# Spatial gating in fp16 halves, and the latents' squares added on VectorE ahead of one fp32 product

## The reference, cut to what matters

```
def _rmsnorm(x, g):
    xf = x.astype(jnp.float32)
    y = xf * lax.rsqrt(jnp.mean(xf * xf, -1, keepdims=True) + EPS)
    return (y * g.astype(jnp.float32)).astype(x.dtype)
...
def _gmlp(u, v, ln_g, ln_b, ws, bs):
    u = jax.nn.gelu(u)
    v = _layernorm(jax.nn.gelu(v), ln_g, ln_b)
    w = jnp.where(jnp.tril(jnp.ones((L, L), dtype=bool)), ws[:, :L, :L], 0).astype(v.dtype)
    vc = v.reshape(B, nc, L, GMLP_GROUPS, GMLP_DG)
    sp = jnp.einsum('gts,bcsgd->bctgd', w, vc) + bs[:, :L].T[:, :, None].astype(v.dtype)
    return u * sp.reshape(B, T, GMLP_WIDTH), v
```

## Time and profile before

| | |
|---|---|
| median of the timed runs | 997.51 us |
| the profiled execution's own time | 998.19 us |
| its span, first to last instruction | 996.3 us |
| TensorE busy | 959.4 us (96%) |
| VectorE busy | 823.3 us (83%) |
| ScalarE busy | 673.0 us (68%) |
| mean granted TensorE clock | 0.996 |

### The profile page before, as it was taken

The page is one execution under the profiler, slowest core; times in us unless marked ns, Lnnn a source line. Parts: engine busy times, 40 slices in busy tenths (PEclk is TensorE's granted clock), DMA queues, the critical chain, the costliest instruction groups (busy, mean ns, idle before and its releaser), DMA issues.

```text
span 996.3 us, 24157 instructions
## 1 busy us (share of the span) xinstructions
PE 959.4 (96%) x9862; PEld 748.8 (75%) x9862; DVE 823.3 (83%) x1484; ACT 673.0 (68%) x1092; POOL 0.7 (0%) x10
## 2 busy tenths in 40 slices
PE   9999999999999899999999999999999989999994
PEld 7877777777776799965578777777777768999652
DVE  6796767776789899998888876678768889999986
ACT  7665555866365899886677545568653659998764
POOL 0000000000000000000000000000000000000000
PEclk9999999999999999999999999999999999999998
DMA  9855444323564299998736544443344425999951
GB/s 366 335 170 160 136 152 129 130 86 128 169 221 141 87 368 379 379 364 299 265 108 233 175 121 142 154 130 95 119 146 151 155 79 177 384 374 397 367 208 56
DMA packets 59651, 205.01 MB, mean 206 GB/s; under 512 B 7216, under 2 KB 10348, under 8 KB 59020
## 3 DMA queue, kind: packets, MB, share of 16 engines
q1 hardware_dynamic: 56748, 198.08, 57.1%
q10 hardware_dynamic: 2784, 5.28, 1.6%
HBM read 198.76 MB, written 3.40 MB: 203 GB/s over the span
## 4 chain that ended last, share of the span: by engine, by line
PE 65%; DVE 18%; ACT 8%; issue 5%; DVEq 2%; DMA 1%; ACTq 0%; SPq 0%
PE bank L1880 42%; DVE wlo L1135 9%; PE bank L1904 4%; ACT whi L593 4%; PE bank L2425 3%; DVE xT L1148 2%; PE bank L1909 1%; PE bank L2242 1%; DVE xlo L1154 1%; PE bank L2441 1%; PE bank L1949 1%; DVEq L1186 1%; PE bank L2174 1%; DVE mu_var L1187 1%; PE bank L2345 1%
## 5 line engine op out<-in xcount | busy, mean ns | idle before, releaser
L1135 DVE SCALAR_TENSOR_TENSOR wlo<-w,whi 128x1024 f16<-128x1024 f32 x358 | 428.1, 1217 | 61.5 <-ACT whi L593 60.2
L593 ACT ACTIVATE whi<-w 128x1024 f16<-128x1024 f32 x358 | 370.0, 1050 | 79.2 <-PE bank L1880 52.9
L1880 PE MATMUL bank<-xhi,whi 128*128 128x320 f16 x688 | 206.1, 300 | 0.8 <-DVE wlo L1135 0.8
L1880 PE MATMUL bank<-xhi,wlo 128*128 128x320 f16 x688 | 205.7, 299 | 0.0
L1880 PE MATMUL bank<-xlo,whi 128*128 128x320 f16 x688 | 205.7, 299 | 0.0
L1880 PE MATMUL bank<-arena_b,whi 128*128 128x112 f16 x2048 | 159.4, 213 | 3.4 <-DVE wlo L1135 3.2
L1880 PE MATMUL bank<-arena_b,wlo 128*128 128x112 f16 x1024 | 156.0, 213 | 0.0
L1880 PEld LDWEIGHTS bank<-arena_b,whi 128*128 128x128 f16 x2048 | 149.8, 98 | 5.3 <-issue 3.1
L1880 PEld LDWEIGHTS bank<-arena_b,wlo 128*128 128x128 f16 x1024 | 100.2, 98 | 0.4 <-issue 0.4
L1880 PEld LDWEIGHTS bank<-xhi,whi 128*128 128x128 f16 x688 | 67.2, 98 | 28.5 <-DVE wlo L1135 1.1
L1880 PEld LDWEIGHTS bank<-xhi,wlo 128*128 128x128 f16 x688 | 67.3, 98 | 26.2
(11 more groups left out here) (377 smaller groups left out, 1755.2 us busy)
## 6 DMA issues: line engine op xcount, KB each, us to landing
w<-in_w SPq DMA_DIRECT2D x358, 512.0 KB, 5.0
arena_b<-head_rows ACTq DMA_DIRECT2D x2, 1920.0 KB, 9.8
rows<-in_rows SPq DMA_DIRECT2D x2, 1024.0 KB, 10.0
xT<-in_x SPq DMA_DIRECT2D x2, 640.0 KB, 5.5
out_y<-xT SPq DMA_DIRECT2D x4, 320.0 KB
out_ckv<-arena_a SPq DMA_DIRECT2D x2, 320.0 KB
acc<-kr SPq DMA_DIRECT2D x2, 288.0 KB
arena_c<-kr SPq DMA_DIRECT2D x2, 288.0 KB
```

What stands on the lines that cost most here:

```text
L593: A(whi[:, n % SLOTS, :], w32[:, n % RAW, :], ACT.Copy, scale=WS).then_inc(hi_done.sem, 1)
L1135: V.scalar_tensor_tensor(wlo[:, n % SLOTS, :], w32[:, n % RAW, :], WS, whi[:, n % SLOTS, :], ALU.mult, ALU.subtract).then_inc(lo_done.sem, 1)
L1880: ins = M(out, w[:, s, sub * P:(sub + 1) * P], rhs(part, k), start=(n == 0), stop=(n == 3 * len(subs) - 1))
```

## The change

There are two parts. In the front, DVE adds the two squares of each latent into one tile, and TensorE does one fp32 product for each latent in place of two; it waits for the new signal `sq_s`. The additions stand at the head of DVE's loop over the token blocks. In the heads, `ws_t` is split once a layer into `ws_hi` and `ws_lo` (after the mask), and `vg` for each head into `vg_hi` and `vg_lo`; TensorE does nine fp16 products in place of three fp32 ones. ACT makes `vg_hi` ahead of `hi_m(5)`, and DVE makes `vg_lo` behind `lo_m(5)`. The bias is now added with the scale 1/256 in the same instruction.

```diff
@@ latents_hi, ACT
                           scale=XS).then_inc(c_hi.sem, 1)
+                        act.wait_ge(ws_masked.sem, ws_masked.value(l, 1))
+                        A(ws_hi[:, :], ws_t[:, :], ACT.Copy, scale=WS).then_inc(ws_h.sem, 1)
                         act.wait_ge(z_norm.sem, z_norm.value(l, 2))
@@ heads, ACT
                         latents_out()
                     for j in range(3):
+                        if j == 0:
+                            act.wait_ge(vg_done.sem, vg_done.value(l, h + 1))
+                            A(vg_hi[:, 0:2, :], vg[:, 0:2, :], ACT.Copy, scale=XS)
+                            A(vg_hi[0:TS, 2, :], vg[0:TS, 2, :], ACT.Copy, scale=XS).then_inc(vg_h.sem, 1)
                         hi_m(5 + j)
@@ front, DVE
                 for i in range(4):
+                    if i == 0:
+                        for k in range(2):
+                            dve.wait_ge(sq_c.sem, sq_c.value(l, k + 1))
+                            V.tensor_tensor(ysq[:, 2 * k, :], ysq[:, 2 * k, :], ysq[:, 2 * k + 1, :], ALU.add
+                                            ).then_inc(sq_s.sem, 1)
                     if i < 3:
                         lo_lead(6 + i)
@@ latents_lo, DVE (last lines)
+                        dve.wait_ge(ws_h.sem, ws_h.value(l, 1))
+                        V.scalar_tensor_tensor(ws_lo[:, :], ws_t[:, :], WS, ws_hi[:, :], ALU.mult, ALU.subtract
+                                               ).then_inc(ws_l.sem, 1)
@@ heads, DVE
                     V.tensor_copy(gvt[0:TS, 2, bass.ds(h * P, P)], vg[0:TS, 2, :]).then_inc(vg_done.sem, 1)
                     lo_m(5)
+                    dve.wait_ge(vg_h.sem, vg_h.value(l, h + 1))
+                    V.scalar_tensor_tensor(vg_lo[:, 0:2, :], vg[:, 0:2, :], XS, vg_hi[:, 0:2, :], ALU.mult,
+                                           ALU.subtract)
+                    V.scalar_tensor_tensor(vg_lo[0:TS, 2, :], vg[0:TS, 2, :], XS, vg_hi[0:TS, 2, :], ALU.mult,
+                                           ALU.subtract).then_inc(vg_l.sem, 1)
...
-                    V.tensor_tensor(gout[:, TP:T], bank[6][:, TP:T], bs_h[:, 0:TS], ALU.add)
+                    V.scalar_tensor_tensor(gout[:, TP:T], bank[6][:, TP:T], UN, bs_h[:, 0:TS], ALU.mult, ALU.add)
@@ front, PE
                         for k in range(2):
-                            pe.wait_ge(sq_c.sem, sq_c.value(l, k + 1))
-                            for c in range(2):
-                                a = M(bank[4 + k][:, 0:T], ones_dm[:, :], ysq[:, 2 * k + c, :],
-                                      start=(c == 0), stop=(c == 1))
-                            a.then_inc(rms_ps.sem, 1)
+                            pe.wait_ge(sq_s.sem, sq_s.value(l, k + 1))
+                            M(bank[4 + k][:, 0:T], ones_dm[:, :], ysq[:, 2 * k, :], start=True, stop=True
+                              ).then_inc(rms_ps.sem, 1)
@@ heads, PE
-                    pe.wait_ge(vg_done.sem, vg_done.value(l, h + 1))
-                    pe.wait_ge(ws_masked.sem, ws_masked.value(l, 1))
+                    pe.wait_ge(vg_l.sem, vg_l.value(l, h + 1))
+                    pe.wait_ge(ws_l.sem, ws_l.value(l, 1))
                     for i, (t0, n) in enumerate(TILES):
                         off = h * P
-                        a = M(bank[6][:, t0:t0 + n], vg[0:n, i, :], ws_t[0:n, bass.ds(off, n)],
-                              start=True, stop=True)
+                        for v, w in ((vg_hi, ws_hi), (vg_hi, ws_lo), (vg_lo, ws_hi)):
+                            a = M(bank[6][:, t0:t0 + n], v[0:n, i, :], w[0:n, bass.ds(off, n)],
+                                  start=(v is vg_hi and w is ws_hi), stop=(v is vg_lo))
```

More of the change, by code:

```diff
@@ L188, in build_trunk @@
         mats16 = sb("mats16", [P, 3, P], F16)
+        ws_hi = sb("ws_hi", [P, 4 * P], F16)
+        ws_lo = sb("ws_lo", [P, 4 * P], F16)
         slot_no = sb("slot_no", [P, CAP])
@@ L220, in build_trunk @@
         v_ws = arena_c[:, 15 * P:15 * P + 3 * (DH + 1)].rearrange("p (i n) -> p i n", i=3)
+        vg_hi, vg_lo = (ysq[:, :, :].rearrange("p a t -> p (a t)").bitcast(F16)[
+            :, 3 * P * n:3 * P * (n + 1)].rearrange("p (i n) -> p i n", i=3) for n in range(2))
         mq = sb("mq", [P, T])
@@ L290, in build_trunk @@
         sq_c = sig("sq_c", 2)
+        sq_s = sig("sq_s", 2)
         rms_ps = sig("rms_ps", 2)
@@ L320, in build_trunk @@
         vg_done = sig("vg_done", MH)
+        vg_h = sig("vg_h", MH)
+        vg_l = sig("vg_l", MH)
+        ws_h = sig("ws_h", 1)
+        ws_l = sig("ws_l", 1)
         sp_ps = sig("sp_ps", MH, 1)
@@ L1451, in _ @@
                     bs_h = bs_bc[:, bass.ds(h * P, P)]
-                    V.tensor_tensor(gout[:, 0:TP].rearrange("p (n t) -> p n t", t=P),
-                                    bank[6][:, 0:TP].rearrange("p (n t) -> p n t", t=P),
-                                    bs_h.unsqueeze(1).broadcast_to([P, 2, P]), ALU.add)
-                    V.tensor_tensor(gout[:, TP:T], bank[6][:, TP:T], bs_h[:, 0:TS], ALU.add)
+                    V.scalar_tensor_tensor(gout[:, 0:TP].rearrange("p (n t) -> p n t", t=P),
+                                           bank[6][:, 0:TP].rearrange("p (n t) -> p n t", t=P), UN,
+                                           bs_h.unsqueeze(1).broadcast_to([P, 2, P]), ALU.mult, ALU.add)
+                    V.scalar_tensor_tensor(gout[:, TP:T], bank[6][:, TP:T], UN, bs_h[:, 0:TS], ALU.mult, ALU.add)
                     dve.drain()
```

## The result

The changed kernel takes 1012.33 us (median of 5 runs, 1010.50 to 1013.86) against 997.7 of the kernel before: ratio 1.0147, 95% interval 1.0135 to 1.0159. That is 14.6 us slower. The forecast was 9.95 us slower, with a range that ended at 1009.8. The profiled execution has a span of 1010.5 us against 996.3, 14.1 more, and TensorE is busy for 961.3 us against 959.4.

A forecast was written before the change was run, and what follows sets the result against it. TensorE, busy in 96% of the span, was taken as the bound: 2.76 + 4.92 - 3.28 + 1.75 + 2.0 = +8.15 us, +9.95 with the clock's fall, so 997.51 becomes 1007.5 us; range 1003.2 to 1009.8.

The forecast's parts named there:

- the clock: TensorE's wait for the squares' sums: clock falls in layer 1 only, 3.6 us of work at half rate, +1.8 us.
- falls twice: Rival: the clock falls in the squares' waits of both layers, 1.8 us more, 1009.3 us; chance 0.09.
- The waits for the sums: Front, TensorE waiting for DVE's additions behind the rotary key: +2.76 us in layer 0, +4.92 us in layer 1.
- The gating's saving: Heads: nine fp16 products in about 0.50 us replace three fp32 in 0.91; 0.41 us less a head, -3.28 us.
- the loads set the pace: Heads, old fp32 gating products: six weight loads of 0.19 us each, 1.1 us, are as long as the products.
- the rival: Gating's products save a quarter only: 0.23 us a head, 1.8 us in all, time 1009.0 us; chance 0.03.
- The wait in head 0: TensorE waits for `vg_lo` ahead of head 0's gating products: +1.75 us in layer 0, +2.0 us in layer 1.
- The sum without the clock: Whole kernel: squares' waits, gating's saving and head 0's waits together, +8.15 us; as rival 1005.7 us, chance 0.27.

The follow-up runs named there:

- with the clock held: The changed kernel plus products nobody reads while TensorE waits for the squares' sums; 1007.05 us, ratio 1.0103 to the kernel before.
- squares alone: The kernel before plus only the two additions and single product for each latent, gating left in fp32; 1009.63 us, ratio 1.0125.
- the run of the heads' filler: The kernel before plus only the fp16 gating, with products nobody reads ahead of the gating's wait in head 0; 999.04 us, ratio 1.0016.

## Why the prediction was wrong

The sign was right, and so were the waits; the size was 9.95 us and is 14.6, outside the range, and most of the difference is the clock.

- **The step that failed is the clock.** The prediction put it as "I take it that the clock falls in layer 1 and not in layer 0", at +1.8 us. It fell in both layers, for 6.8 us each and not for 3.6, and cost 5.3 us by the trace and 4.9 in the medians when it was taken away. Three things were misread. The 5.2 us from the last product to the fall at the kernel's end are one instance, and were used as a threshold. Falls came 2.1 us into a wait, and behind a wait of 1.7 us that had ended, and at the changed kernel's own end 2.2 us after the last product. The half-rate stretch at the kernel's start was taken as the length of all such stretches, and was read too short besides: a mean of 299 ns from 5.2 on takes in three slow products, and the starts change from 0.21 to 0.11 us apart only at 5.5, so 4.2 us ran at half rate and not 3.6. And "falls twice" was given 1.8 us more, with 0.09, when both errors point the same way: a wait of 3.7 us was called "well under the one case seen", though one case says little of what lies under it. The Trainium skill ("TensorE: Matmul & The Clock Gate", HAM oscillation) says that a wait between bursts drops the clock and lets each burst start slow. That rule was nearer to what happened than the reading of the trace's single fall, for the waits of 3.8 and 5.9 us.
- **The waits for the sums: right.** Forecast 2.76 and 4.92 us, with the clock held 2.77 and 4.81. Block 6 then starts at 33.17 in layer 0 (33.15 forecast), and TensorE's idle times of 3.84 and 5.86 us are the 3.7 and 5.9 forecast. The additions took 0.49 us each.
- **The gating's saving: forecast too large.** Forecast 0.41 us a head, measured 0.28, so 2.24 in place of 3.28 us. The term that was mis-sized is that of the three products of 64 columns: 0.08 to 0.17 us together were forecast, and the third tile takes 0.29, most of it at the change of rows from 128 to 64 and back. The reading of the old products was wrong too. That "the loads set the pace", since each lasts 0.19 us, doesn't hold: the full-size records start 0.11 us apart, so the loads overlap. A full-size fp32 product costs four times 0.056, and replacing it saves a quarter, as the rival had it. That rival got 0.03; its 0.23 us a head is nearer to the 0.28 than the forecast's 0.41.
- **The wait in head 0: right in kind, a little too large.** Forecast 1.75 and 2.0 us, measured 1.45 and 1.8. The chain from `vg_done` to the first product was 3.5 us forecast; in the trace of the change it runs from 72.31 to 75.75, 3.4. `vg_done` itself comes 7.6 us later than before, 5.2 of it from the front, so 2.4 where 2.35 was forecast. That this delay comes from ACT's wait for the mask was shown by moving it. In heads 1 to 3 nothing waits, as forecast.
- **The sum without the clock: somewhat small.** Forecast 8.15 us; with the clock held it was 8.7 in the spans and 9.7 in the medians. The gating's smaller saving is 1.0 of this, and the shorter waits in the heads gave half a microsecond of it back, which makes the 8.7. The last microsecond between spans and medians lies in the two executions that were profiled: 0.8 us above its median for the kernel before, 0.2 below for the filled one.

## What to carry to other kernels

Work that is taken from the bound engine and handed to one that executes in order arrives when that engine gets to it, not when its inputs are ready: look first at what stands ahead of it in that queue. The same two additions cost 12 us behind the rotary key, with the clock's falls in it, and nothing or up to one in the middle of the decay chain. A new wait of the matmul engine has to be priced with its clock, not only by its length: here 9.7 us of standing still cost another 5 us through the half rate behind it. A wait as long as these, 3.7 us and more, should be priced as if the fall comes; a single fall in a profile is a sample and not a threshold.

## What the runs showed of the hardware

- With every wait of 3.7 to 3.8, 4.4 and 5.9 us that was profiled and not filled (seven, in four profiles) the granted clock fell: 2.1 to 4.7 us after the last product, or in one case (squares alone, layer 0) 1.0 us after the wait had ended. A wait of 2.0 us kept it, in one execution. Behind waits of 1.6 to 1.9 us it fell in some executions, 0.7 to 1.8 us after the wait's end, and not in others. At the kernels' ends it fell 2.2 to 5.3 us after the last product.
- The low stretches inside the kernel were 3.4 or 6.8 us long in all profiles. Products of 128 columns started 0.107 us apart in them (34.37, 34.48 and 34.58 in the changed kernel) and 0.056 otherwise. A low stretch behind a layer norm's wait cost less: at 809 in the run of the heads' filler TensorE fell back by 1.3 us and had won 1.1 of it back eight microseconds later.
- Products nobody reads, sized to the wait, held the clock at 1.00 there.
- An fp16 product of 128 columns with a weight load for each took 0.056 us, and an fp32 one 0.22. Three fp16 products with 64 rows and 64 columns started 0.04 and 0.03 us apart, but 0.15 us passed from the last product with 128 rows to the first of them and 0.12 us from the last of them to the next with 128.
